# Squares of the norms in eight buffers with some sums on VectorE, a new order of the first loads, and four dots ahead of the C groups

## The reference, cut to what matters

```python
for l in range(2):
    mod = silu(c) @ ada_w[l] + ada_b[l]
    sh1, sc1, g1, sh2, sc2, g2 = split(mod, 6)
    h = rms_norm(x, norm_mix_g[l]) * (1 + sc1) + sh1
    x = x + g1 * hybrid_mixer(h, ...)
    h = rms_norm(x, norm_ffn_g[l]) * (1 + sc2) + sh2
    x = x + g2 * peer(h, ...)

def hybrid_mixer(h, ...):
    q, k, v, glu, gates = split(h @ w_in)
    attn = sliding_window_attention(rope(rms_norm(q)), rope(rms_norm(k)), v) @ w_o_attn
    u = causal_depthwise_conv(ga * sigmoid(gb))          # 31 taps
    conv = silu(layer_norm(u, g, b)) @ w_o_conv
    return (sigmoid(g_attn) * attn + sigmoid(g_conv) * conv) @ w_out

def peer(h, ...):    # 8 heads, 16 of 16384 experts each
    top 16 of each half score -> top 16 of their sums -> softmax gates, ids
    y = sum over the experts of gate * gelu(u[id] . h) * v[id]
```

## Time and profile before

| | us |
|---|---|
| median of 3 runs | 3705.74 (3700.5 to 3709.14) |
| the profiled execution's own time | 3699.87 |
| its span in the trace | 3698.1 |
| TensorE matmul busy | 3567.0 (96%) |
| TensorE weight load busy | 3274.7 (89%) |
| VectorE busy | 3102.8 (84%) |
| ScalarE busy | 1581.4 (43%) |
| GpSimd busy | 1387.7 (38%) |
| mean granted TensorE clock | 0.983 of full |

### The profile page before, as it was taken

How to read it: one execution, slowest core, us unless ns; L and a number is a source line. 1 busy time by engine, 2 the same in 40 slices (tenths; PEclk the granted TensorE clock), 3 DMA queues, 4 the chain that set the end, 5 groups by cost and what they waited for, 6 DMA issues and landing times.

```text
span 3698.1 us, 61360 instructions
## 1 busy us (share of the span) xinstructions
PE 3567.0 (96%) x19266; PEld 3274.7 (89%) x19266; DVE 3102.8 (84%) x6294; ACT 1581.4 (43%) x2335; POOL 1387.7 (38%) x1140
## 2 busy tenths in 40 slices
PE   5999999999999999999999999999999999999999
PEld 4766688999999999999977676889999999999999
DVE  6899876997999878888868997679989988788888
ACT  3474424444555433333345634244445554333333
POOL 0000002575556544444400000036655665554553
PEclk9999999999999999999999999999999999999999
DMA  4111272467999899999921122625579998999998
GB/s 188 63 52 60 75 256 94 142 187 237 331 353 335 287 334 347 350 346 349 329 79 58 52 69 94 236 98 165 178 262 349 341 322 295 351 346 348 349 341 295
DMA packets 408601, 863.49 MB, mean 233 GB/s; under 512 B 165520, under 2 KB 231056, under 8 KB 407952
## 3 DMA queue, kind: packets, MB, share of 16 engines
q1 hardware_dynamic: 297456, 539.62, 44.0%
q0 software_dynamic: 73728, 268.47, 20.6%
q10 hardware_dynamic: 37152, 52.45, 3.8%
HBM read 774.41 MB, written 85.98 MB: 233 GB/s over the span
## 4 chain that ended last, share of the span: by engine, by line
issue 50%; PE 28%; POOL 16%; DMA 2%; DVE 2%; POOLq 0%; ACT 0%; DVEq 0%; SPq 0%; ACTq 0%
PE ps L820 8%; PE ps L821 8%; PE ps L822 8%; POOL w_lo L506 7%; POOL gbuf L522 5%; POOL spare L536 4%; PE ps L562 2%; PE ps L560 2%; PE ps L561 2%; DMA raw<-stream 1%; PE ps L794 1%; DMA gbuf<-u_rows,ids_u 1%; DVE oneR L1688 1%; DMA cg<-gelu_scratch 0%; DVE w_lo L1661 0%
## 5 line engine op out<-in xcount | busy, mean ns | idle before, releaser
L877 ACT CAST w_hi<-raw 128x1024 fp32r<-128x1024 f32 x680 | 715.7, 1055 | 901.0 <-DMA raw<-stream 849.9
L560 PE MATMUL ps<-h_hi,w_hi 128*128 128x384 f32 (+1 forms) x2944 | 1066.0, 362 | 19.9 <-DVE w_lo L1661 13.7
L562 PE MATMUL ps<-h_hi,w_lo 128*128 128x384 f32 (+1 forms) x2944 | 1039.9, 353 | 0.0
L561 PE MATMUL ps<-h_lo,w_hi 128*128 128x384 f32 (+1 forms) x2944 | 1039.0, 353 | 0.0
L820 PE MATMUL ps<-cf_hi,w_hi 128*128 128x384 f32 x2048 | 691.1, 337 | 11.9 <-DVE cf_lo L1719 7.9
L821 PE MATMUL ps<-cf_lo,w_hi 128*128 128x384 f32 x2048 | 688.9, 336 | 0.0
L822 PE MATMUL ps<-cf_hi,w_lo 128*128 128x384 f32 x2048 | 688.9, 336 | 0.0
L536 POOL TENSOR_TENSOR spare<-spare 128x1 f32<-128x1 f32 x504 | 344.2, 683 | 857.6 <-DVE y_sp L1704 477.5
L560 PEld LDWEIGHTS ps<-h_hi,w_hi 128*128 128x128 f32 x2944 | 557.2, 189 | 72.6 <-issue 15.4
L561 PEld LDWEIGHTS ps<-h_lo,w_hi 128*128 128x128 f32 x2944 | 557.6, 189 | 38.8 <-issue 5.7
L562 PEld LDWEIGHTS ps<-h_hi,w_lo 128*128 128x128 f32 x2944 | 556.4, 189 | 37.5
(11 more groups left out here) (245 smaller groups left out, 4933.0 us busy)
## 6 DMA issues: line engine op xcount, KB each, us to landing
raw<-stream SPq DMA_DIRECT2D x682, 512.0 KB
gelu_scratch<-g_out ACTq DMA_DIRECT2D x256, 192.0 KB
cg<-gelu_scratch SPq DMA_DIRECT2D x256, 192.0 KB
c_scratch<-stage SPq DMA_DIRECT2D x64, 512.0 KB
cg<-c_scratch SPq DMA_DIRECT2D x256, 128.0 KB
qT<-ada SPq DMA_DIRECT2D x32, 512.0 KB
cgate<-ada SPq DMA_DIRECT2D x32, 512.0 KB, 6.7
w_rows<-ada SPq DMA_DIRECT2D x32, 512.0 KB, 7.1
```

Source lines behind the costliest of these rows:

```text
L560: nc.tensor.matmul(ps[:, b, 0:n], wh, hi[:, c, t0:T], start=c == 0, stop=False)
L561: nc.tensor.matmul(ps[:, b, 0:n], wh, lo[:, c, t0:T], start=False, stop=False)
L562: mm = nc.tensor.matmul(ps[:, b, 0:n], wl, hi[:, c, t0:T], start=False, stop=c == C - 1)
L877: nc.scalar.copy(w_hi[:, s], raw[:, s]).then_inc(hi_done, 1)
```

## The change

It makes these edits. The launch issues the rows 0 to 11 ahead of x and the parameters, and the two weight tiles before the last two rows; VectorE takes the parameters before row 12 and makes the two low parts before row 14; TensorE sums all eight chunks of squares at launch, before the loop. For the next layer's norm the sums move to the end of the loop's body: three chunks as they are and a sum of five by VectorE (four adds), and the cast and low part of tile 1 move ahead of the last updates of `xT`. The convolution norm squares into eight buffers, VectorE adds the last four, TensorE does five sums, and the second late gate is read after chunk 1. At the second norm each square follows its chunk's update on ScalarE's queue, between the casts of the output projection; the issue of `keys` stays behind the casts of tiles 63 and 64 and with that comes behind the squares of chunks 0 and 1. VectorE adds squares 1 to 6 to square 0 and TensorE does two sums. `first_pair` waits for the high part of a chunk, does the four matmuls that need only that, waits for the low part and does the last two. `GATHER_TILE` goes from 16 to 20, `DOTS_FIRST` from 6 to 4 and `DOTS_BY_GROUP` from 112 to 114, and one more low part stands after the second dot. The diff, without the declarations of semaphores and with lines dedented:

```diff
...
 SLOTS = 4
-GATHER_TILE = 16
+GATHER_TILE = 20
 ADA_ALL = 6 * C
...
 ROW4 = PAIRS[1][0] * TOPK // 4 - PAIRS[1][0]
-DOTS_FIRST, DOTS_BY_GROUP = 6, 112
+DOTS_FIRST, DOTS_BY_GROUP = 4, 114
 TOP_STEPS = RH * 45 + NB * 65 + 2
...
 GATE_TAPS = 7
+ADDED = {5: (1, 2, 3, 4), 6: (5,)}
 MIDDLE_LOADS = {54: (0, 1), 56: (2, 3), 58: (4, 5, 6), 60: (7, 8, 9, 10), 62: (11, 12, 13, 14),
...
 ada_in = [sem(f"ada_in{s}") for s in range(4)]
...
     sp.dma_start(cact[:], c_d.broadcast_to([P, D])).then_inc(c_in, 16)
-    sp.dma_start(xT[:], x_d).then_inc(x_in, 16)
-    sp.dma_start(params[:], params_d).then_inc(const_in, 16)
     for n in range(ADA_1):
-        if n >= 12 and n % 2 == 0:
-            sp.dma_start(raw[:, n // 2 - 6], stream[n // 2 - 6]).then_inc(loaded[n // 2 - 6], 16)
-        sp.dma_start(rows0[:, n], ada[n]).then_inc(ada_in[n // 4], 16)
+        if n == 12:
+            sp.dma_start(xT[:], x_d).then_inc(x_in, 16)
+            sp.dma_start(params[:], params_d).then_inc(const_in, 16)
+        if n == 14:
+            for i in range(2):
+                sp.dma_start(raw[:, i], stream[i]).then_inc(loaded[i], 16)
+        sp.dma_start(rows0[:, n], ada[n]).then_inc(ada_in[n // 4] if n < 14 else last_rows, 16)
     sp.wait_ge(primed, 1)
...
     pe.wait_ge(rope_in, 32)
+    def token_sums(b, squares, first, last):
+        for tt in range(NB):
+            mm = nc.tensor.matmul(ps[:, b, 2 * tt:2 * tt + 2], squares[:, tt * P:(tt + 1) * P],
+                                  mean[:, 0:2], start=first and tt == 0, stop=last and tt == NB - 1)
+        return mm
+    for c in range(C):
+        pe.wait_ge(sqx_done, c + 1)
+        mm = token_sums(0, x_squares[:, c], c == 0, c == C - 1)
+    mm.then_inc(sqx_used, 1)
     with pe.Fori(0, DEPTH) as l:
...
-        def first_pair(i, hi, lo, chunks):
+        def first_pair(i, hi, lo, highs, chunks):
...
             for c in range(C):
+                pe.wait_ge(highs[0], highs[1] + c + 1)
+                for q in range(2):
+                    nc.tensor.matmul(ps[:, q], w_hi[:, (i + q) % 4, c], hi[:, c], start=c == 0, stop=False)
+                    nc.tensor.matmul(ps[:, q], w_lo[:, (i + q) % 4, c], hi[:, c], start=False, stop=False)
                 pe.wait_ge(chunks[0], chunks[1] + c + 1)
                 for q in range(2):
-                    wh, wl = w_hi[:, (i + q) % 4, c], w_lo[:, (i + q) % 4, c]
-                    nc.tensor.matmul(ps[:, q], wh, hi[:, c], start=c == 0, stop=False)
-                    nc.tensor.matmul(ps[:, q], wh, lo[:, c], start=False, stop=False)
-                    mm = nc.tensor.matmul(ps[:, q], wl, hi[:, c], start=False, stop=c == C - 1)
+                    mm = nc.tensor.matmul(ps[:, q], w_hi[:, (i + q) % 4, c], lo[:, c], start=False, stop=c == C - 1)
                     if c == C - 1:
...
-        def token_sums(b, squares, first, last):
-            for tt in range(NB):
-                mm = nc.tensor.matmul(ps[:, b, 2 * tt:2 * tt + 2], squares[:, tt * P:(tt + 1) * P],
-                                      mean[:, 0:2], start=first and tt == 0, stop=last and tt == NB - 1)
-            return mm
         def spread(b, k):
...
-        for c in range(5):
-            if c < 4:
-                pe.wait_ge(sqx_done, l * C + c + 1)
-            else:
-                pe.wait_ge(sqx_sum, 3 * l + 3)
-            mm = token_sums(0, x_squares[:, c], c == 0, c == 4)
-        mm.then_inc(sqx_used, 1)
         spread(7, 2 * l)
...
-        first_pair(0, h_hi, h_lo, (h_ready, 2 * l * C))
+        first_pair(0, h_hi, h_lo, (hhi_done, 2 * l * C), (h_ready, 2 * l * C))
         for i in range(2, I_Q + C):
...
         proj(I_CG + 2, h_hi, h_lo)
-        for c in range(C):
-            pe.wait_ge(ln_sq, l * C + c + 1)
-            nc.tensor.matmul(ps[:, 6], mean, sq[:, c % 2], start=c == 0, stop=c == C - 1).then_inc(ln_mm, 1)
+        for c in range(5):
+            if c < 4:
+                pe.wait_ge(ln_sq, l * C + c + 1)
+            else:
+                pe.wait_ge(ln_sum, 3 * l + 3)
+            nc.tensor.matmul(ps[:, 6], mean, x_squares[:, c], start=c == 0, stop=c == 4).then_inc(ln_mm, 1)
         proj(I_CG + 3, h_hi, h_lo)
-        first_pair(I_CG + FIRST_GATES, n_hi, n_lo, (ln_lo, l * C))
+        first_pair(I_CG + FIRST_GATES, n_hi, n_lo, (ln_hi, l * C), (ln_lo, l * C))
         for m in range(2, FIRST_GATES):
...
         proj_loop(I_OUT + 4, I_QRY, o_hi, o_lo)
-        for c in range(C):
-            pe.wait_ge(sq_done, l * C + c + 1)
-            token_sums(7, sq[:, c % 2], c == 0, c == C - 1).then_inc(sq_used, 1)
+        pe.wait_ge(sq_added, l * (C - 2) + C - 2)
+        token_sums(7, x_squares[:, 0], True, False)
+        pe.wait_ge(sq_done, l * C + C)
+        token_sums(7, x_squares[:, C - 1], False, True).then_inc(sq_used, 1)
         spread(6, 2 * l + 1)
...
-        first_pair(I_QRY, h_hi, h_lo, (h_ready, 2 * l * C + C))
+        first_pair(I_QRY, h_hi, h_lo, (hhi_done, 2 * l * C + C), (h_ready, 2 * l * C + C))
         half_scores(0)
...
             experts(s, l * NKEYS + j, l * NT + I_W + j, False, s == 3)
+        for c in range(4):
+            if c < 3:
+                pe.wait_ge(sqx_done, (l + 1) * C + c + 1)
+            else:
+                pe.wait_ge(sqx_sum, 4 * l + 4)
+            mm = token_sums(0, x_squares[:, c], c == 0, c == 3)
+        mm.then_inc(sqx_used, 1)
...
             act.wait_ge(ln_step, l * LN_STEPS + c + 1)
-            if c >= 2:
-                act.wait_ge(ln_mm, l * 2 * C + C + c - 1)
-            nc.scalar.activation(sq[:, c % 2], yT[:, c], ACT.Square).then_inc(ln_sq, 1)
+            nc.scalar.activation(x_squares[:, c], yT[:, c], ACT.Square).then_inc(ln_sq, 1)
...
         high_at(I_CG + 5)
-        act.wait_ge(ln_mm, l * 2 * C + 2 * C)
+        act.wait_ge(ln_mm, (l + 1) * (C + 5))
         nc.scalar.activation(rstd[:], ps[:, 6], ACT.Sqrt, bias=eps_k).then_inc(ln_root, 1)
...
             nc.scalar.copy(n_hi[:, c], hs[:, c % 2]).then_inc(ln_hi, 1)
-            if c in (0, 2):
-                late_gate_read(2 + (0, 2).index(c))
+            if c < 2:
+                late_gate_read(2 + c)
         for m in range(2, FIRST_GATES):
...
             nc.scalar.copy(o_hi[:, m], hx[:, m % 2]).then_inc(mrg_hi, 1)
+        def updated_square(c):
+            act.wait_ge(bank_read[c % 2], read_no(I_OUT + c))
+            nc.scalar.activation(x_squares[:, c], xT[:, c], ACT.Square).then_inc(sq_done, 1)
         ll = act.snap(l + 0)
+        root_table()
         for i in range(I_OUT, I_QRY):
             high_at(i + 2)
+            if i > I_OUT:
+                updated_square(i - 1 - I_OUT)
             if i == I_OUT + 2:
...
                 act.dma_start(keys[:], keys_d[ll]).then_inc(key_in, 16)
-        root_table()
-        for c in range(C):
-            act.wait_ge(bank_read[c % 2], read_no(I_OUT + c))
-            if c >= 2:
-                act.wait_ge(sq_used, l * C + c - 1)
-            nc.scalar.activation(sq[:, c % 2], xT[:, c], ACT.Square).then_inc(sq_done, 1)
-        act.wait_ge(sq_used, (l + 1) * C)
+        updated_square(C - 1)
+        act.wait_ge(sq_used, l + 1)
         token_root(7)
...
         root_table()
+        high_at(NT + 1)
         for c in range(C):
...
             squares_of_x(c)
-        high_at(NT + 1)
...
     starts = [(bank_read[0], 1), (bank_read[1], 1), (g_st[0], 16), (g_st[1], 16), (tile_done, 4),
-              (c_mm, 4), (c_ev, 4), (cf_ready, 4), (c_st, 64), (row_used, 4), (mod_step, 1), (mod_add, 1), (x_upd, C), (primed, 1)]
+              (c_mm, 4), (c_ev, 4), (cf_ready, 4), (c_st, 64), (row_used, 4), (ada_in[3], 32), (mod_step, 1), (mod_add, 1), (x_upd, C), (primed, 1)]
     for n, (counter, start) in enumerate(starts):
...
-    dve.wait_ge(const_in, 16)
-    parameters(slice(0, 1))
-    def sum_squares(counted):
-        dve.wait_ge(sqx_done, (counted + 1) * C)
-        nc.vector.tensor_tensor(x_squares[:, 4], x_squares[:, 4], x_squares[:, 5], ALU.add).then_inc(sqx_sum, 1)
-        nc.vector.tensor_tensor(x_squares[:, 6], x_squares[:, 6], x_squares[:, 7], ALU.add).then_inc(sqx_sum, 1)
-        dve.wait_ge(sqx_sum, 3 * counted + 2)
-        nc.vector.tensor_tensor(x_squares[:, 4], x_squares[:, 4], x_squares[:, 6], ALU.add).then_inc(sqx_sum, 1)
+    def sum_squares():
+        for n, c in enumerate((3, 5)):
+            dve.wait_ge(sqx_done, (l + 1) * C + c + 2)
+            nc.vector.tensor_tensor(x_squares[:, c], x_squares[:, c], x_squares[:, c + 1],
+                                    ALU.add).then_inc(sqx_sum, 1)
+        dve.wait_ge(sqx_done, (l + 1) * C + C)
+        dve.wait_ge(sqx_sum, 4 * l + 2)
+        nc.vector.tensor_tensor(x_squares[:, 5], x_squares[:, 5], x_squares[:, 7], ALU.add).then_inc(sqx_sum, 1)
+        dve.wait_ge(sqx_sum, 4 * l + 3)
+        nc.vector.tensor_tensor(x_squares[:, 3], x_squares[:, 3], x_squares[:, 5], ALU.add).then_inc(sqx_sum, 1)
...
             dve.wait_ge(ada_in[n // 4], 64)
+        if n == 12:
```

(36 more changed lines are left out.)

3 lines of the change are left out of this document (added).

## The result

The changed kernel takes 3664.48 us (median of 4 runs, 3659.42 to 3673.5) against 3703.12 us of the kernel before on the same chip: ratio 0.9899, 95% interval 0.9885 to 0.9913, so 32 to 43 us faster. The profiled execution took 3664.64 us with a span of 3662.8 (before 3699.87 and 3698.1), so span against span it is 35.3 us. The forecast was 46.9 us and 3659, with a range of 3645 to 3680. The sign and the range held; the question is where 11.6 us of the sum went.

A forecast was written before the change was run, and what follows sets the result against it. TensorE, busy in 96% of the span, bounds the kernel. Launch -1.4, layers -43.4, turn -3.1 and tail +1.0 sum to -46.9 us; allowing for the profiled execution being 5.9 under the median, 3659 us, range 3645 to 3680.

The forecast's parts named there:

- Launch: Before the first pair: rows ahead of x, eight sums until 42.3 us bound the reciprocal; 0.7 us won, 1.4 with high first.
- High part first: First pairs start on the high chunk alone: 0.7 us at each of four token norms, nothing at the convolution norm.
- Convolution norm: Five sums bring the root 2.4 us earlier, the second late gate read moves 1.4 us: 3.8 us a layer.
- Second norm: Behind the output projection, two token sums after the last tile instead of eight: 7.2 us a layer.
- Keys: Output projection: keys issued later, behind chunk 1's square, delay what shares their transfer time; 1.2 us a layer charged as loss.
- Gathers and dots: U tiles: stalls at tiles 20 and 43 go, first C group 11.2 us earlier a layer, 3.5 of it from gathers.
- The lock variant: Within the 0.21 rival: VectorE's instructions shut GpSimd out, tile 21 is late by 3.5 us a layer, 7 in all: 3666.
- Turn: Between the layers: three sums before the loop's turn, one behind four adds; root earlier by 2.6, less 0.2: 2.4 us.
- Tail: End of the last layer: later updates, four adds and a sum that nothing reads end the span; 1.0 us lost.
- long stretches have no gaps: Whole kernel: TensorE busy in 96% of the span, time to win only at waits, helper sums or the lower clock.
- given back in the u tiles: Rival, chance 0.21: VectorE is the next late engine in the C groups; sum about 36 us, 3670.
- The slow one: Rival, chance 0.03: ScalarE's queue in the output projection stalls TensorE at each of 16 tiles: 3706 at 2.9 us a tile.

The follow-up runs named there:

- best: Changed kernel with keys ahead of chunk 1's square, last sum atop the loop, two VectorE adds and six sums at launch, next layer's tile-1 low part later: 3655.23 us.
- low_with_high: Changed kernel, but each first pair waits for both high and low chunk before its matmuls: 3668.03 us, one run.
- gates_early: Changed kernel with late gate reads earlier, gate 2 before the wait for the sums, gate 3 behind chunk 0: 3663.87 us, ratio 0.9898.
- last_sum: Changed kernel with the last token sum at the top of the layer loop and four launch adds on GpSimd: 3663.47 us, ratio 0.9886.

## Why the prediction was right in sign and range, and 8 to 12 us too large

- **Launch**: right (-1.7 for -1.4), and for the reason given: sums until 42.3, VectorE ready at 39.2. `best` shows the cost of that choice, 2.5 us.
- **High part first**: the 0.7 us are real at the pair (0.8 in `low_with_high`). Wrong was "nothing at the convolution norm" and silence on what follows: a wait of 0.54 us behind the pair of each layer's first norm (none behind that of the second) and 0.5 us more at the tile behind the convolution's pair. Of 2.8 us about 0.7 remain: four times 0.7 less two times 0.54 and two times 0.5.
- **Convolution norm**: root 2.4 earlier and gate read 1.5 earlier, both as worked out, 3.9 together; less the 0.54 that makes 3.4, and the stage from the first pair to the restart became 3.6 and 3.0 us shorter. Undone, it costs 4.2 and 3.0. The next limit, named in no step, is the Silu chain (`gates_early`).
- **Second norm**: 7.2 forecast; undoing it and the late keys together costs 6.6 (6.0 against the mean of the sixteen late stages), so 6.3 to 6.9 with the keys at 0.3.
- **Keys**: the charge of 1.2 us a layer was too high; 0.3, inside the scatter. (The 2.4 us from which it was halved is itself short: 1 MB is 2.6 us at the prediction's own 1.29 for 512 KB.) By the prediction's estimate from the rule of the Trainium skill, DMA: Bandwidth & Descriptors, section on queues, rings and completion order (each DMA engine takes turns between queues), the loss would have been 2.4 us; no run here shows that.
- **Gathers and dots**: 11.2 forecast, 10.7 measured, split 2.7 and 8 and not 3.5 and 7.7. The lock variant asked for 3.5 us at tile 21; there is no wait there.
- **Turn**: the sum left 0.2 us for TensorE's turn of the loop. The root did come 2.2 us earlier (2.6 worked out), but from root to spread it takes 1.86 us (1857.70 - 1855.84) where it took 0.88: 1.0 us exposed.
- **Tail**: 1.9 for 1.0: VectorE's updates start 1.4 us behind the transpose of chunk 0 (3652.55 and 3651.14), where it was 0.3, so 1.1 later and not 0.7, and the last sum took 1.87.
- **What failed most** is a stage that the prediction did not price. It held that TensorE's "long stretches have no gaps", from one profiled execution whose v tiles ran at 537.3 and 537.1 us. Even there TensorE waited 1.32 us in the v tiles of layer 0, and 0.70 and 1.52 in those of layer 1. In the 20 such stages of the changed kernel and the nine kernels made from it that load the rows of `ada` at the same places, they ran from 535.3 to 545.4 us, mean 539.9: 5 us more over two layers. Part of this was in the forecast unknowingly, as the 5.9 us by which the profiled execution was under the median. Of the miss by the medians, 8.3 us (46.9 less 38.6), the terms above make about 3.6: order of the pair 2.1, turn 1.1, tail 0.9, second norm 0.6, gathers and dots 1.0, less 1.8 for the keys and 0.3 for the launch. The other 4 to 5 are open; with the rows left out of both kernels 3 of them vanish by the medians and all by the ratios, and they lie inside the interval of 32 to 43.
- **The rivals**: "given back in the u tiles" named about the right size, 36, by a mechanism that did not happen: no C group waits over 1.4 us, and TensorE's waits for `oneR` behind the first group grew by 0.4 us over the two layers. The lock variant's 3666 lies nearest to the measured 3664.5, by luck: it needs 3.5 us at tile 21. The slow one did not happen either: TensorE's waits in the output projection are 0.5 us in the profile after, and 1.7 at most in the others (`last_sum`).

## What to carry to other kernels

Take the floor of a stage from several executions where its transfers are full: one profile without a wait says little. When a wait is removed at a restart, look for the chain two tiles behind it; a start ahead of it (here by 1.7 us) is given back there. Undoing one part at a time and comparing stages between fixed instructions measured edits of 2 us that the totals, which scatter by 8, could not.

## What the hardware showed that was not expected

- While GpSimd added squares (7.01 us for four of 128x512), VectorE's multiplications of 128x1024 took 2.27 and 2.29 us in place of 1.22, and the copy of the parameters 0.86 in place of 0.34. This bears out what the Trainium skill, SBUF — State Buffer, section on who interferes with whom, says on the port pair that VectorE and GpSimd share: operations of VectorE with two inputs in SBUF contend with GpSimd's reads, and a copy can when it runs in a mode with two ports. In which mode this copy ran no trace here shows.
- TensorE's idle time at its turn of the loop over layers is not one number: 1.12 us; 1.9 us ahead of the spread in the changed kernel (1.7 to 2.7 over the kernels here), where 0.92 stands at spreads with no turn ahead, and also at launch, where the loop is entered; 2.9 and 3.3 us where a sum is the first thing in the loop (`last_sum`, `best`), which starts 0.9 and 2.3 us after its adds are done.
- In the v tiles the DMA share is 0.99 to 1.00 at 334 to 339 GB/s, where the launch moves 408 at 1.02. In the v tiles a weight tile made ScalarE wait 11.47 us, and removing 4% of the bytes took 12.1 us off one kernel and 6.9 off the other. Four rows (2 MB) issued together behind the first v tile made a wait of 0.66 to 4.91 us in 18 of 22 profiled stages.
- The lower clock behind a wait comes or stays out. Behind the same 2.24 us at tile 20 the granted clock was 0.50 from 758 to 760 us in one layer, and 1.00 in the other; the stage was 3.7 us longer in the one and 1.7 in the other.
